# Second block of a two-block transformer: decays on ScalarE and GpSimd, inverse roots on VectorE by shift and Newton steps, values centred ahead of the retention, index scores moved

## The reference

```python
z = rmsnorm(x, norm1_w) @ w_in            # qa 512 | latent kv 128 | index q 4x32, k 32, w 4 | qb, kb, vb, gb 512 each
# "a" half: 8 heads with one shared key and value, 64 keys chosen for each query
score = sum_h(iw * relu(iq_h . ik) * scale); score = where(admissible, score, -inf)
_, idx = top_k(score, 64)
logits = rmsnorm(qa) . k[idx] * dh ** -0.5 + bias; out_a = softmax(logits) @ v[idx]
# "b" half: retention with 8 heads, in chunks of 64 tokens
scores = einsum('bihd,bjhd->bhij', q, k) * inner_decay       # 0 where j > i
new_state = state * chunk_decay + einsum('bjhd,bjhe->bhde', k * key_decay, v)
# group norm of each head over its 64 columns (mean and variance, GN_EPS), gain and bias, * silu(gb)
out = concat(out_a, out_b) @ w_out
```

## Time and profile before

| | |
|---|---|
| median of 3 runs | 978.34 us |
| profiled execution | 978.28 us, span 976.6 us |
| PE busy | 938.0 us (96%), mean granted clock 0.99 |
| DVE busy | 587.7 us (60%) |
| ACT busy | 476.0 us (49%) |
| POOL busy | 70.8 us (7%) |
| stage of the change | about 675 to 773 us of the span |

### The profile page before, as it was taken

How to read it: one execution, slowest core, us unless ns; L and a number is a source line. 1 busy time by engine, 2 the same in 40 slices (tenths; PEclk the granted TensorE clock), 3 DMA queues, 4 the chain that set the end, 5 groups by cost and what they waited for, 6 DMA issues and landing times.

```text
span 976.6 us, 13275 instructions
## 1 busy us (share of the span) xinstructions
PE 938.0 (96%) x4758; PEld 790.2 (81%) x4758; DVE 587.7 (60%) x801; ACT 476.0 (49%) x699; POOL 70.8 (7%) x132
## 2 busy tenths in 40 slices
PE   5999989999999999999999999999897999999998
PEld 4788778888888887778888888888776888888887
DVE  3777766756565576543856555558887374545543
ACT  4765565544444365562744444446335364344341
POOL 2101030100000010001100000002133000000000
PEclk9999999999999999899999999999898999999999
DMA  8844223765655443221765565555332055555551
GB/s 278 298 143 132 87 92 131 258 209 174 201 185 191 154 172 130 87 87 45 258 217 193 176 207 178 167 181 191 113 108 85 3 178 199 182 181 198 179 172 43
DMA packets 95435, 157.77 MB, mean 162 GB/s; under 512 B 5928, under 2 KB 37624, under 8 KB 95392
## 3 DMA queue, kind: packets, MB, share of 16 engines
q1 hardware_dynamic: 93872, 155.09, 47.7%
q10 hardware_dynamic: 1488, 2.10, 0.7%
q0 software_dynamic: 32, 0.02, 0.0%
HBM read 156.12 MB, written 1.06 MB: 161 GB/s over the span
## 4 chain that ended last, share of the span: by engine, by line
PE 85%; DVE 6%; ACT 4%; POOL 2%; issue 2%; DMA 1%; SPq 0%; ACTq 0%; DVEq 0%; POOLq 0%
PE proj L1405 8%; PE proj L1407 8%; PE proj L1406 8%; PE turn L1445 5%; PE score L1405 5%; PE proj L1445 5%; PE score L1406 5%; PE score L1407 5%; PE outp L1405 5%; PE outp L1407 5%; PE outp L1406 5%; PE proj L1449 3%; PE turn L1449 3%; PE turn L1432 2%; PE score L1569 2%
## 5 line engine op out<-in xcount | busy, mean ns | idle before, releaser
L1693 DVE TENSOR_TENSOR wlo<-raw,whi 128x2048 fp32r<-128x2048 f32 x145 | 329.7, 2278 | 221.5 <-ACT whi L1194 147.6
L1194 ACT ACTIVATE whi<-raw 128x2048 fp32r<-128x2048 f32 x64 | 122.6, 1916 | 170.0 <-PE outp L1407 57.5
L1405 PE MATMUL proj<-whi,set 128*128 128x512 f32 (+1 forms) x432 | 174.7, 404 | 9.8 <-DVE wlo L1693 7.0
L1188 ACT ACTIVATE whi<-raw 128x2048 fp32r<-128x2048 f32 (+1 forms) x81 | 153.0, 1901 | 47.6 <-PE outp L1407 18.4
L1407 PE MATMUL proj<-whi,set 128*128 128x512 f32 (+1 forms) x432 | 169.5, 392 | 0.0
L1406 PE MATMUL proj<-wlo,set 128*128 128x512 f32 (+1 forms) x432 | 169.2, 392 | 0.0
L1405 PEld LDWEIGHTS proj<-whi,set 128*128 128x128 f32 x432 | 83.0, 192 | 27.1 <-issue 9.2
L1407 PEld LDWEIGHTS proj<-whi,set 128*128 128x128 f32 x432 | 82.6, 191 | 17.6
L1406 PEld LDWEIGHTS proj<-wlo,set 128*128 128x128 f32 x432 | 83.1, 192 | 15.6
L1405 PE MATMUL score<-whi,set 128*128 128x512 f32 x236 | 92.8, 393 | 0.4 <-ACT e L1331 0.4
L1405 PE MATMUL outp<-whi,set 128*128 128x512 f32 x236 | 92.8, 393 | 0.4 <-issue 0.4
(11 more groups left out here) (207 smaller groups left out, 1240.0 us busy)
## 6 DMA issues: line engine op xcount, KB each, us to landing
raw<-in_a_w_up SPq DMA_DIRECT2D x32, 512.0 KB, 4.3
raw<-in_a_w_down SPq DMA_DIRECT2D x32, 512.0 KB, 4.5
raw<-in_b_w_up SPq DMA_DIRECT2D x32, 512.0 KB, 4.2
raw<-in_b_w_down SPq DMA_DIRECT2D x32, 512.0 KB, 4.4
raw<-in_w_gate SPq DMA_DIRECT2D x22, 512.0 KB, 4.0
raw<-in_w_up SPq DMA_DIRECT2D x22, 512.0 KB, 4.9
raw<-in_w_down SPq DMA_DIRECT2D x22, 512.0 KB, 3.9
raw<-in_a_w_in SPq DMA_DIRECT2D x20, 512.0 KB, 6.6
```

The lines of the kernel that those rows point to most:

```text
L1188: act.activation(shaped(whi, u), shaped(raw, u), ACT.Copy).then_inc(hi_done, 1)
L1194: act.activation(shaped(whi, u), shaped(raw, u), ACT.Copy).then_inc(hi_done, 1)
L1405: pe.matmul(out_, hi, wh, start=start, stop=False)
L1693: dve.tensor_tensor(shaped(wlo, u), shaped(raw, u), shaped(whi, u), ALU.subtract).then_inc(lo_done, 1)
```

## The change

Scores of the retention are now scaled by ACT into `ret` (one buffer pair in rope_tmp, one in e, by turns) and the 128x128 blocks on the diagonal masked by POOL's affine_select. The means of the heads are taken from v before the retention in place of from its output after it. The three inverse roots of this stage run on DVE in place of POOL: a shift and a subtraction on the bits give the first value, and three Newton steps follow, 12 instructions for a norm. The normalising steps of gain, bias and gate of both tiles are on DVE. In the list the second index scores, the splits of vb to ua, the first half of the selection, the transposes of qa and of the gated half, and the second half of the selection have other places. INDEX_BLOCK puts the index queries in blocks of qk that the queries of qa take later.

```diff
+        ret = [[rt[:, 0, :], rt[:, 1, 0:TOK]], [e[:, 0, :], e[:, 1, 0:TOK]]]
...
-        INDEX_BLOCK = [8, 10, 9, 11]
+        INDEX_BLOCK = [0, 2, 1, 3]
...
-        sn_use = half_around(turn_small, qb, 1, 0, xb[1], "O")
+        sn_use = multiply_around(turn_small, qb[1], 0, UK, xb[1], "O", False, True)
...
         va_need = (kava_done, 1)
         step("index_sum", i0)
         step("shared_key_sum", kava)
+        split(qb[1] + AHEAD)
         tile(vb, 0, 1, xb)
-        split(vb[0] + AHEAD)
-        i1 = index_scores(1)
         kb_use = turn_heads(zq[:, 1], [0, 1, 2, 3], heads(0, 4, 4), rope_ready(rk.rope))[-1]
         zfree[1] = kb_use + 1
-        step("index_sum", i1)
         tile(vb, 1, 0, xb)
-        select(i0, 0, 4)
-        step("shared_key_norm", kava)
         qb_use = turn_heads(zq[:, 0], [0, 1, 2, 3], pairs(0, Q_QB, 4), rope_ready(rq.rope))[-1]
         zfree[0] = qb_use + 1
+        i1 = index_scores(1)
+        step("shared_key_norm", kava)
+        step("index_sum", i1)
         tile(vb, 1, 1, xb)
-        split(vb[1] + AHEAD)
         ev = evacuate(vb[1], [((0, 512), lambda t: v[:, t, 0:512])], rs_2)
-        vr_need = (chunk_evac, 2 * ev.chunk + 2)
-
-        retention_scores(0, rope_ready(rq.rope)(1))
+        center = add("center_values")
+        center.chunk, center.mu = ev.chunk, col(16)
+        vr_need = (v_centered, 2)
+
+        retention_scores(0)
+        split(vb[0] + AHEAD)
         tile(qa, 0, 0, xb)
+        select(i0, 0, 4)
         r = retention_out(0)
-        retention_scores(1, r)
+        retention_scores(1)
         select(i0, 4, 8)
         tile(qa, 0, 1, xb)
-        split(qa[0] + AHEAD)
+        split(vb[1] + AHEAD)
         r = retention_out(1)
-        retention_scores(2, r)
+        retention_scores(2)
         ka_use = turn_heads(sn[:, :, 0, :].rearrange("p t n -> p t n"), [0], pairs(0, Q_KA, 1),
                             lambda t: (ka_done, t + 1))[-1]
         tile(qa, 1, 0, xb)
         r = retention_out(2)
-        retention_scores(3, r)
+        retention_scores(3)
+        split(qa[0] + AHEAD)
         select(i1, 0, 4)
         tile(qa, 1, 1, xb)
         ev = evacuate(qa[1], [((0, 512), lambda t: zq[:, 0, t, :])], rs_2, slot_free=zfree[0])
         qn = add("query_norm")
         qn.chunk, qn.ss, qn.rs = ev.chunk, col(16), col(16)
-        split(qa[1] + AHEAD)
         last = retention_out(3)
-        group = add("group_center")
-        group.o, group.mu, group.va, group.rs = last[1], col(16), col(16), col(16)
+        group = add("group_square")
+        group.o, group.va, group.rs = last[1], col(16), col(16)
         step("query_scale", qn)
         tile(gb, 0, 0, xb)
-        step("group_sum", group)
+        step("group_scale", group)
         tile(gb, 0, 1, xb)
-        split(gb[0] + AHEAD)
-        tile(gb, 1, 0, xb)
+        split(qa[1] + AHEAD)
         qa_use = turn_heads(zq[:, 0], [0, 1, 2, 3], heads(0, 0, 4), lambda t: (qn_done, t + 1))[-1]
         zfree[0] = qa_use + 1
         st = add("gain_load")
         st.free = zfree[0]
+        tile(gb, 1, 0, xb)
+        step("group_gain", group)
         tile(gb, 1, 1, xb)
+        evacuate(gb[1], [((0, 512), lambda t: zq[:, 1, t, :])], rs_2, slot_free=zfree[1], silu=True)
+        group.gate = (chunk_evac, 2 * count.chunk - 1)
+        step("group_gate", group)
 
         d = [idx_item(0, 0), idx_item(1, 0)]
-        step("group_scale", group)
-        step("group_gain", group)
         mix(d[0]); mix(d[1])
-        evacuate(gb[1], [((0, 512), lambda t: zq[:, 1, t, :])], rs_2, slot_free=zfree[1], silu=True)
-        group.gate = (chunk_evac, 2 * count.chunk)
+        ua, ub, uc, ud = out_units(A["w_out_2"][0], (512, 0))
+        o2 = turn_operand(o_nat, 1, [(None, 1, UK)], (ob_done, 2), 0)[-1]
         turn_weights(d[0]); turn_weights(d[1])
         d += [idx_item(2, 0), idx_item(3, 0)]
-        step("group_gate", group)
+        mix(d[2]); mix(d[3])
+        multiply(ua, 1, UK, o2, "P", True, False, hold=True, tiles=[0])
         attend(d[0], va_need); attend(d[1], va_need)
-        mix(d[2]); mix(d[3])
-        ua, ub, uc, ud = out_units(A["w_out_2"][0], (512, 0))
-        o2 = turn_operand(o_nat, 1, [(None, 1, UK)], (ob_done, 2), 0)[-1]
         select(i1, 4, 8)
         split(gb[1] + AHEAD)
-        multiply(ua, 1, UK, o2, "P", True, False, hold=True, tiles=[0])
         turn_weights(d[2]); turn_weights(d[3])
         d += [idx_item(0, 1), idx_item(1, 1)]
         attend(d[2], va_need); attend(d[3], va_need)
...
-                elif st.kind == "query_norm":
-                    inverse_of_sums(st.rs, st.ss, DH)
+                elif st.kind == "retention_scores":
+                    for a in range(2):
+                        n = TOK - a * P
+                        pool.wait_ge(decayed, 2 * st.p + a + 1)
+                        block = ret[st.p % 2][a].rearrange("p (c n) -> p c n", c=2)[:, :, 0:P]
+                        pool.affine_select(out=block, in_=block, compare_op=ALU.is_ge, fill=0.0, base=0,
+                                           pattern=[[0, 2], [1, P]], channel_multiplier=-1).then_inc(masked, 1)
...
-                elif st.kind == "group_gate":
-                    y = o_nat[:, 0, 512:1024]
...
-                    pool.tensor_tensor(y, y, zq[:, 1, 0, :], ALU.mult).then_inc(ob_done, 1)
...
+                elif st.kind == "retention_scores":
+                    for a, (s, _) in enumerate(st.banks):
+                        act.wait_ge(s_full, s + 1)
+                        n = TOK - a * P
+                        if st.p > 1:
+                            act.wait_ge(o_full, ret_out[st.p - 2] + 1)
+                        elif st.p == 0:
+                            act.wait_ge(rope_done, 2 * rq.rope + 2)
+                        else:
+                            act.wait_ge(bias_stored, 16)
+                        for c in range(2):
+                            h = 2 * st.p + c
+                            ins = act.activation(ret[st.p % 2][a][:, c * n:(c + 1) * n], Sb[s % 2][:, c * n:(c + 1) * n],
+                                                 ACT.Copy, scale=dec[:, a, 8 + h:9 + h])
+                        ins.then_inc(decayed, 1)
...
+            def inverse_rms(dst, ss, n, eps):
+                width = dst.shape[1]
+                var, r2 = newton_dve[:, 0, 0:width], newton_dve[:, 1, 0:width]
+                behind(dve.tensor_scalar(var, ss, 1.0 / n, eps, ALU.mult, ALU.add))
+                bits, half = dst.bitcast(I32), r2.bitcast(I32)
+                behind(dve.tensor_scalar(half, var.bitcast(I32), 1, None, ALU.logical_shift_right))
+                behind(dve.tensor_scalar(bits, half, -1.0, float(0x5f3759df), ALU.mult, ALU.add))
+                for _ in range(3):
+                    behind(dve.tensor_tensor(r2, dst, dst, ALU.mult))
+                    behind(dve.scalar_tensor_tensor(out=r2, in0=r2, scalar=-0.5, in1=var, op0=ALU.mult, op1=ALU.mult))
+                    behind(dve.scalar_tensor_tensor(out=dst, in0=r2, scalar=1.5, in1=dst, op0=ALU.add, op1=ALU.mult))
...
-                    ins.then_inc(sum_done, 1)
+                    behind(ins)
+                    inverse_rms(st.rs, st.ss, DH, EPS)
...
-                elif st.kind == "retention_scores":
-                    for a, (s, _) in enumerate(st.banks):
-                        dve.wait_ge(s_full, s + 1)
-                        n = TOK - a * P
-                        dve.wait_ge(*st.after)
-                        for c in range(2):
-                            h = 2 * st.p + c
-                            o = c * n
-                            dst, src = rt[:, a, o:o + n], Sb[s % 2][:, o:o + n]
-                            ins = dve.scalar_tensor_tensor(out=dst[:, 0:P], in0=src[:, 0:P],
-                                                           scalar=dec[:, a, 8 + h:9 + h], in1=tri[:], op0=ALU.mult,
-                                                           op1=ALU.mult)
-                            if n > P:
-                                ins = dve.tensor_scalar(dst[:, P:n], src[:, P:n], dec[:, a, 8 + h:9 + h], None,
-                                                        ALU.mult)
-                        ins.then_inc(decayed, 1)
...
-                elif st.kind == "group_center":
-                    dve.wait_ge(o_evac, st.o)
-                    for t in range(NT):
-                        y, mu = heads_view(o_nat[:, t, 512:1024]), st.mu[:, 8 * t:8 * t + 8]
+                elif st.kind == "center_values":
+                    for t in range(NT):
+                        dve.wait_ge(chunk_evac, 2 * st.chunk + t + 1)
+                        y, mu = heads_view(v[:, t, 0:512]), st.mu[:, 8 * t:8 * t + 8]
                         behind(dve.tensor_reduce(mu, y, AX_X, ALU.add))
                         behind(dve.tensor_scalar(mu, mu, 1.0 / DH, None, ALU.mult))
-                        dve.tensor_tensor(y, y, spread(mu, DH), ALU.subtract).then_inc(yc_done, 1)
```

(44 more changed lines are left out.)

22 lines of the change are left out of this document (9 added, 13 removed).

## The result

The changed kernel takes 981.46 us (median of 7 runs, 979.8 to 983.23), the one before 977.67 us in the same comparison (7 runs, 976.38 to 979.02). The ratio is 1.0035, 95% interval 1.0025 to 1.0044: slower by 3.8 us as the medians go. The prediction said 982.7 us, 4.4 above its 978.28. The profiled execution after took 981.46 us, with a span of 979.7 us; it is 3.2 us longer than the one of before, and the last transposes of the stage stand 3.2 us later. The first index scores, with which the stage begins on PE, stand 0.2 us later (676.42, not 676.21), so the stage holds the other 3.0.

What follows compares the result with a forecast made beforehand. PE bounds the kernel, busy 938.0 of 976.6 us; only its waits and lower clock can change. Later second-tile scores (+2.1) and a third low-clock stretch (+2.3) add 4.4 to 978.28: 982.7 us, range 976.0 to 987.0.

Steps and rivals of the forecast that it cites:

- The early wait: Ahead of qb's transposes: the 2.55 us wait and its low clock go; PE is through the next tile 5.9 us earlier.
- Decays and masks: Retention scores: ACT's decays stand beside PE's tiles; POOL's masks cost PE 0.4 us in all, 2.2 at the outer end.
- the port rule: VectorE and GpSimd lock shared ports: the third pair's mask would stand until gb[0]'s split ends, the sum 0.4 us higher.
- qa's norm: Transposes of qa start at 722.6, 4.8 us earlier, after a 4.4 us wait; its 2.2 us clock loss hides in the next.
- The gated half: Transposes of the gated half start at 735.3, 7.3 us earlier, with 1.8 us of waiting for DVE's group norm and gates.
- The weights: Transposes of the attention weights start at 739.0 after 2.9 us of idle, with 2.9 us more lost at the lower clock.
- the selection's wait: Ahead of the second tile's scores: PE waits 4.2 us for the selection's second half; scores at 752.9, 2.1 us later.
- The tail: Second tile's scores to last transposes: 21.12 us before, plus 2.3 for a third low-clock stretch, ending at 776.3.
- the first: Rival: the wait of 2.9 us ahead of the weights leaves the clock up; 979.8 us, chance 0.16.
- The second: Rival: the clock stays up behind the wait ahead of the weights and the wait of 4.2 us; 977.5 us, chance 0.12.
- the third: Rival: faster, as DVE's chain from last split to gates is at least 2.5 us shorter; about 976.0 us, chance 0.15.
- the fourth: Rival: masks are held up each time, four of eight costing PE 0.4 to 0.8 us more; 984.5 to 986.5, chance 0.10.

Runs made afterwards that it cites:

- the tile put ahead: The changed kernel with one tile of gb[1] ahead of qa's transposes again: 982.32 us, ratio 1.0034 to the kernel before.
- Work in the wait: The changed kernel with a tile's 12 matmuls more, result unused, in the 4.27 us wait ahead of the second token tile's scores: 979.44 us, ratio 1.0013.
- the fastest version: Against the version with both selection moves, the lower part of ua's split goes behind o2's and the first two maxima ahead of the gate: 969.88 us, ratio 0.9916.
- the version with both selection moves: The changed kernel with the second selection's first half ahead of gb[1]'s split and its second half ahead of a tile: 971.74 us, ratio 0.9932.

## Why the prediction was right

The direction, the place and the size were right: 982.7 us forecast and 981.46 measured, or 4.4 us more forecast against 3.8 (medians) and 3.2 (profiles). The mechanism held at each step, but the starts of the gated half and of the selection came out nearer than their terms were, because errors cancelled. Step by step:

- The early wait: foreseen to go with its clock, and it went. The first retention output was forecast at 695.0 with 1.6 us of wait; it is at 695.08 with 1.36.
- Decays and masks. One affine_select took 0.41 us, as taken (0.4), and the two of a pair 0.92 with the gap between. For PE I had 0.4 us in all. POOL's timeline:

```profile
698.50 0.92 POOL L1169 TENSOR_SCALAR_AFFINE_SELECT e<-e 128x256 f32<-128x256 f32 x2 [6.13 <-ACT e L1370]
703.90 2.42 POOL L1169 TENSOR_SCALAR_AFFINE_SELECT rope_tmp<-rope_tmp 128x256 f32<-128x256 f32 x2 [4.48 <-ACT rope_tmp L1370]
```

  DVE's split ran from 703.41 to 705.69 and the third pair's two masks took 2.42 us, those of the other pairs 0.92. This is the case that the port rule of the Trainium skill ("SBUF — State Buffer", section "SBUF: two separate sides") speaks of, and the trace agrees with it. The retention output behind started at 706.42, 0.1 us behind the mask's end, and PE lost about 0.2 us, less than the 0.8 that the rule would have made of it, since the tile ahead covered the rest. With the centring behind the retention the third pair's masks and the split start together; there they took 2.91 us and PE waited 0.54.
- qa's norm: forecast 722.6 with 4.4 us of wait, measured 723.21 with 4.33. The 0.6 us lie at the chain's start: the fourth pair's scores were done at 709.06 and not 708.35, since six steps of 1.28 to 1.39 stand behind 695.08 (three outputs and three times scores), and the sum had five. From there each term of the chain fits its row. The Newton steps took 0.21 us each, as the row of a small step said. That the wait and its clock are hidden in the next one was shown by the tile put ahead: same time.
- The gated half: forecast 735.3, measured 735.05. Part of this is luck: the chain began 0.6 us late, and the reduction of the squares took 1.27 us where the sum has 1.8 (723.2 to 725.0), so the two cancel. What was wrong besides is the split between wait and work: PE's own scores ended at 734.7, not 733.5, because the transposes began 0.6 us later and the low stretch behind 4.33 us of idle cost 2.6 us (723.21 to 732.36 is 9.15 for 6.5 us of work) and not 2.2. Neither cost anything in the end.
- The weights: forecast 739.0, measured 738.43. The stretch at the lower clock behind was 3.4 us long, where those of before were 6.8, and cost some 1.5 us: the scores from 739.28 took 3.8 us where the first two items' took 2.3 from 732.36. My sum had 2.9. This is the mis-sized term. The other work up to the selection's wait took 7.5 us and not 6.8, which hides half of that. The selection so began at 747.21 and not 748.8, took 0.3 us more than the 4.1 of the sum, and the second tile's scores came at 751.67 in place of 752.9: the 1.2 us between forecast and result.
- The tail: 775.16 - 751.67 = 23.49 us against 21.12 in before, 2.37 more; forecast 2.3. Work in the wait took 2.27 of it away, as it should by this reading.
- The rivals: the first (the clock stays up behind the wait ahead of the weights) fell, but the clock's loss there was 1.5 us and not 2.9, so half of its difference came. The second and the third fell, and so did the fourth: the masks of one pair of four were held up, and cost little. The fourth's own sum was a little high besides: four times 0.4 to 0.8 on 982.7 makes 984.3 to 985.9, not 984.5 to 986.5.

What the prediction did not see is how little separates the change from a gain. Its parts are each worth something in this order: by the medians the decays' offload is worth 4.1 us (with the masks left on GpSimd), the roots on VectorE 3.1, the centring 2.7. Two steps of the list, the halves of the second selection, cost 3.95 and 6.88 us, more than the whole difference.

## What to carry to other kernels

Where every engine walks one hand-written list, look in the trace for an engine's idle time whose next item waits for another engine while an item behind it is ready; exchanging the two is free (3.6 us of DVE here). Count a wait of PE of some 4 us at 6 to 7, since the lower clock behind cost 1.6 to 2.6 more here, but count it only if the next wait does not take it in. Offloading an engine pays where that engine releases the next step of the chain; look, too, at what will run beside the work in its new place, as the masks beside a split show (0.92 us alone, 2.42 to 2.91 beside it).

## What the runs showed of the chip

The granted clock did not follow from the length of a wait alone. In the fastest version PE waited 1.39 us ahead of the first retention output and the clock fell 2 us later for 3.4 us; in the version with both selection moves the same wait was 1.34 us, with the same work around, and it stayed up. Windows of the two, the fastest version first:

```profile
695.00:696.00 1.00, 1.00 (x8) 0.95 (x8) 1.00 (x1) 0.00 (x0) 0.00 (x0) 0.97 0.00 0
696.00:697.00 1.00, 1.00 (x5) 0.82 (x4) 0.93 (x5) 0.16 (x1) 0.00 (x0) 0.50 0.00 0
```

```profile
697.00:698.00 1.00, 1.00 (x9) 0.92 (x8) 1.00 (x2) 0.00 (x0) 0.00 (x0) 1.00 0.00 0
698.00:699.00 1.00, 1.00 (x8) 0.93 (x7) 0.90 (x5) 0.60 (x2) 0.00 (x0) 1.00 0.00 0
```

The Trainium skill ("TensorE: Matmul & The Clock Gate", "Part 1: The HAM clock gate") says that the monitor behind the clock runs free of the kernel, so that the same kernel can meet it at another phase; the two profiles agree with that, and no run here shows it alone. The price of a wait varied too. Behind the wait of 4.33 us ahead of qa's transposes the lower level held for 6.8 us in the changed kernel and cost 2.6, and behind the same wait with the centring behind it held for 3.4 and cost 1.6 (8.1 us for 6.5 of work). Behind 2.28 us it held for 3.4 (738.43, after), behind 2.55 and 3.46 us of before for 6.8 each. So a wait of 1.4 to 2.6 us was a risk of nothing to 3.2 us, not a sure cost, and a sum over such waits needs a range for each.
